# Two-layer hybrid encoder on one core: a new written-out order for the attention stage, with the first output tiles inside it

## What is computed

```python
xn = rms_norm(h, attn_norm_g[l])
q, k, v, u = jnp.split(xn @ w_in[l], splits, axis=-1)        # 512, 128, 128, 512 columns
q = apply_rope(rms_norm(q, q_norm_g[l]), cos, sin) * q_scale  # 8 heads of 64
k = apply_rope(rms_norm(k, k_norm_g[l]), cos, sin)            # 2 heads of 64
attn = sliding_sink_attention(q, k, v, sinks[l])              # chunks of 64, window 128, 16 global keys
pool = multiscale_pool(u, w_pool[l], pool_scale[l])           # 4 groups: trailing mean of 2/4/8/16 minus the token,
                                                              # then a 128x128 map for each group
h = h + jnp.concatenate([attn, pool], axis=-1) @ w_out[l]
xn = rms_norm(h, ffn_norm_g[l])                               # second sub-layer, not touched
h = h + (gelu(causal_dwconv(xn @ w_gate[l])) * (xn @ w_up[l])) @ w_down[l]
```

## Time and profile before

| | before |
|---|---|
| median of 3 runs | 1080.35 us (1080.12 to 1081.51) |
| the profiled execution's own time | 1079.61 us |
| its span | 1077.8 us |
| PE busy | 1044.7 us (97%) |
| PEld busy | 995.3 us (92%) |
| DVE busy | 683.9 us (63%) |
| ACT busy | 461.7 us (43%) |
| POOL busy | 106.5 us (10%) |
| mean granted TensorE clock | 0.988 of full speed |
| DMA | 94.94 MB, mean 88 GB/s |

### The profile page before, as it was taken

The page is one execution under the profiler, slowest core; times in us unless marked ns, Lnnn a source line. Parts: engine busy times, 40 slices in busy tenths (PEclk is TensorE's granted clock), DMA queues, the critical chain, the costliest instruction groups (busy, mean ns, idle before and its releaser), DMA issues.

```text
span 1077.8 us, 18641 instructions
## 1 busy us (share of the span) xinstructions
PE 1044.7 (97%) x7880; PEld 995.3 (92%) x7880; DVE 683.9 (63%) x1008; ACT 461.7 (43%) x698; POOL 106.5 (10%) x108
## 2 busy tenths in 40 slices
PE   7998899999999999999999988999999999999998
PEld 7887799999999999999999878999989999899987
DVE  6667645658946689455546576546698466984452
ACT  6775445334323343233338655354343333433322
POOL 1262000010000100000002610001000000000000
PEclk9989999999999999999999899999999999999999
DMA  7211222332232322322231112332313323133312
GB/s 231 80 49 40 79 79 79 92 105 79 79 118 80 118 79 79 118 79 88 89 99 40 50 40 79 100 97 78 114 44 118 118 84 112 41 123 113 98 59 78
DMA packets 94106, 94.94 MB, mean 88 GB/s; under 512 B 3424, under 2 KB 92856, under 8 KB 94024
## 3 DMA queue, kind: packets, MB, share of 16 engines
q1 hardware_dynamic: 93456, 93.58, 27.2%
q10 hardware_dynamic: 312, 0.18, 0.1%
q0 software_dynamic: 256, 0.01, 0.0%
HBM read 91.65 MB, written 2.10 MB: 87 GB/s over the span
## 4 chain that ended last, share of the span: by engine, by line
PE 78%; DVE 11%; ACT 8%; issue 3%; DMA 0%; POOL 0%; DVEq 0%; SPq 0%; ACTq 0%; POOLq 0%
PE slot L577 63%; PE slot L865 11%; ACT probs L1213 3%; PE slot L625 1%; ACT rot_s L1135 1%; DVE w_lo L430 1%; ACT w_hi L419 1%; DVE nmax L1550 1%; PE slot L925 1%; DVE h L1757 1%; DVE ms_work L1495 1%; DVE probs L1569 1%; DVE v_T L1470 1%; DVE mix_lo L1585 1%; DVE m_op_lo L1721 0%
## 5 line engine op out<-in xcount | busy, mean ns | idle before, releaser
L577 PE MATMUL slot<-x_hi,w_hi 128*128 128x264 f32 (+2 forms) x1520 | 355.9, 301 | 4.2 <-DVE u_sb L1532 2.9
L577 PE MATMUL slot<-x_lo,w_hi 128*128 128x264 f32 (+2 forms) x1520 | 352.3, 298 | 0.0
L577 PE MATMUL slot<-x_hi,w_lo 128*128 128x264 f32 (+2 forms) x1520 | 351.9, 298 | 0.0
L577 PEld LDWEIGHTS slot<-x_hi,w_hi 128*128 128x128 f32 x1520 | 248.1, 190 | 16.7 <-DVE u_sb L1532 4.3
L577 PEld LDWEIGHTS slot<-x_lo,w_hi 128*128 128x128 f32 x1520 | 246.7, 190 | 7.3
L577 PEld LDWEIGHTS slot<-x_hi,w_lo 128*128 128x128 f32 x1520 | 246.4, 190 | 7.5
L430 DVE TENSOR_TENSOR w_lo<-raw,w_hi 128x2048 fp32r<-128x2048 f32 (+1 forms) x70 | 157.2, 2246 | 90.0 <-ACT w_hi L419 90.0
L419 ACT ACTIVATE w_hi<-raw 128x2048 fp32r<-128x2048 f32 (+3 forms) x72 | 128.2, 1781 | 162.2 <-PE slot L577 113.3
L1029 POOL TENSOR_TENSOR work<-work 128x528 f32<-128x528 f32 (+1 forms) x32 | 41.9, 1309 | 712.3 <-DVE work L1681 350.6
L1283 ACT ACTIVATE work<-gate,par_all 128x528 f32<-128x528 f32 (+1 forms) x44 | 31.9, 731 | 135.1 <-DVE gate L1451 68.2
L865 PE MATMUL slot<-m_op_hi,w_hi 128*128 128x264 f32 (+1 forms) x256 | 73.8, 288 | 1.2 <-DVE h L1757 0.8
(11 more groups left out here) (195 smaller groups left out, 1627.8 us busy)
## 6 DMA issues: line engine op xcount, KB each, us to landing
raw<-in_w_gate SPq DMA_DIRECT2D x44, 512.0 KB, 4.7
raw<-in_w_up SPq DMA_DIRECT2D x44, 512.0 KB, 4.4
raw<-in_w_down SPq DMA_DIRECT2D x32, 512.0 KB, 4.2
raw<-in_w_in SPq DMA_DIRECT2D x19, 512.0 KB, 4.8
raw<-in_w_out SPq DMA_DIRECT2D x16, 512.0 KB, 4.0
raw<-in_w_down SPq DMA_DIRECT2D x16, 384.0 KB, 3.6
x_in<-in_x SPq DMA_DIRECT2D x4, 512.0 KB, 6.1
out<-y_out SPq DMA_DIRECT2D x4, 256.0 KB, 2.3
```

Of the source, the lines that this page charges most:

```text
L577: ins = nc.tensor.matmul(out_part, w[ws][:, r, cols], a[:, k, tokens], start=first and n == 0 and w is w_hi and a is a_hi, stop=end and w ...
```

## The change

The arithmetic is the same; the order in which PE, ACT and DVE do it is another, and it is written out call by call where loops and tables stood.

- **PE, ahead of attention.** Layer 1: rows 6 and 7 of k come with the first two rows of v between the products with the high and the low part of x. q1 moves to slot 0 and its first rows (three in layer 0, one in layer 1) go ahead of the transposes of v. u3's last rows mix with the first six rows of the side work.
- **PE, attention.** scores run one to three blocks ahead of the transposes; a transpose and the heads before it are no longer adjacent but have rows of side work between them; the side tiles and the pooling maps, now in halves (m3a to m0b), alternate between two spare areas, one in slot 2 and one in slot 3. The transposed meta columns move to a place in slot 3's first bank (`meta_T`), so probs_T(b) also waits for heads(b-2) to be read out.
- **PE, output.** Tiles out0 and out1 are cut into ten parts (`OUT_PARTS`), done among the last blocks; rows of heads 0 to 4 cover the first half of the tokens. Output unit 0 is split in two halves of rows on ACT and DVE.
- **ACT.** The order is by call: squares of q2, shift(3), squares of q3, split_hi of unit 4, q_rms(0), shift(4), q_rms(1), then the blocks. exps waits for the row maxima alone and does the sink's exponential last. Pooling maps are read out in halves.
- **DVE.** The order is by call; the one chain semaphore becomes two (`nm_steps`, `rden_steps`).

```diff
+FILL = [("u2a", KT), ("u2b", KT), ("u1a", KT), ("m3a", 1), ("m3b", 1), ("u1b", KT), ("u0a", KT), ("u0b", KT), ("m2a",
+        1), ("m2b", 1), ("m1a", 1), ("m1b", 1), ("m0a", 1), ("m0b", 1)]
+OUT_PARTS = [(0, (7, 6), (0, 1)), (0, (0, 1, 2, 3), (0,)), (1, (7, 6), (0, 1)), (1, (0, 1, 2, 3), (0,)), (0, (5,), (0, 1)),
+             (1, (5,), (0, 1)), (0, (4,), (0, 1)), (1, (4,), (0, 1)), (0, (0, 1, 2, 3), (1,)), (1, (0, 1, 2, 3), (1,))]
...
-        side = slot[3][:, 1, 0:HALF]
+        area = {4: slot[3][:, 1, 0:HALF], 5: slot[2][:, 1, 0:HALF]}
+        meta_T = slot[3][:, 0, 4 * CHUNK:4 * CHUNK + P]
...
                 if l > 0:
-                    project("k", U_KV, ready=lambda k: pe.wait_ge(xlo_ready, l * (2 * KT) + (k + 1)))
-                    project("v", U_KV)
+                    s = open_slot("k", l)
+                    pe.wait_ge(lo_split[U_KV % 2], slot_turn(l, U_KV) + 2)
+                    dense(s, U_KV % 2, 0, eight[0:6], x_hi, x_lo, last=False,
+                          ready=lambda k: pe.wait_ge(xlo_ready, l * (2 * KT) + (k + 1)))
+                    sv = open_slot("v", l)
+                    for part in (0, 1):
+                        if part == 1:
+                            dense(sv, U_KV % 2, P, eight[0:2], x_hi, x_lo, last=False)
+                        for k in (6, 7):
+                            pe.wait_ge((xhi_ready, xlo_ready)[part], l * (2 * KT) + (k + 1))
...
                 project("q0", U_Q)
+                s, ahead = open_slot("q1", l), 3 if l == 0 else 1
+                dense(s, U_Q % 2, P, eight[0:ahead], x_hi, x_lo, last=False)
                 s = open_slot("v_T", l)
...
                 column_mean("k_sq", l, block_mean, k_squares, headsq_ready, l * 5 + 1)
-                project("q1", U_Q)
+                dense(ps.slot("q1"), U_Q % 2, P, eight[ahead:], x_hi, x_lo, first=False).then_inc(filled[ps.slot("q1")], 1)
                 project("q2", U_Q + 1)
                 project("q3", U_Q + 1)
-                q_means(0)
-                project("u3", U_U23)
...
                     if b > 1:
                         pe.wait_ge(meta_out, l * (NB - 1) + (b - 1))
+                    if b > 1:
+                        pe.wait_ge(evac[ps.slot(f"heads{b - 2}")], ps.before(f"heads{b - 2}", l) + 1)
...
-                project_side(*side_rows(-1))
-                q_means(1)
-                for step in range(NB + 2):
-                    if step < NB:
-                        scores(step)
...
+                q_means(0)
+                u3_rows(0, 6)
+                fill(0, 2)
+                u3_rows(6, 7)
+                fill(2, 3)
+                u3_rows(7, 8)
+                fill(3, 6)
+                q_means(1)
+                scores(0)
+                fill(6, 8)
+                scores(1)
+                fill(8, 14)
+                scores(2)
+                fill(14, 16)
+                probs_T(0)
+                scores(3)
+                fill(16, 20)
+                probs_T(1)
+                fill(20, 25)
+                heads(0)
+                fill(25, 26)
+                scores(4)
...
+                fill(48, 51)
+                heads(4)
+                fill(51, 52)
+                probs_T(6)
+                fill(52, 53)
+                heads(5)
+                fill(53, 54)
+                fill_out(0)
+                probs_T(7)
+                fill(54, 55)
+                heads(6)
+                fill_out(1)
+                fill_out(2)
+                probs_T(8)
+                fill(55, 56)
+                heads(7)
+                fill_out(3)
+                fill_out(4)
+                heads(8)
+                fill_out(5)
+                fill_out(6)
+                fill_out(7)
+                fill_out(8)
+                fill_out(9)
...
-                    act.wait_ge(nm_ready, l * NB + b + 1)
+                    act.wait_ge(nm_steps, 3 * (l * NB + b) + 3)
...
-                shift(3)
-                split_hi(act, l, 4)
-                q_squares(2)
-                q_rms(0)
-                q_squares(3)
-                shift(4)
-                q_rms(1)
...
+                q_squares(2)
+                shift(3)
+                q_squares(3)
+                split_hi(act, l, U_U01)
+                q_rms(0)
+                shift(4)
+                q_rms(1)
+                exps(0)
+                exps(1)
...
+                split_lo(dve, l, U_U01)
+                scaled("u3", u_sb[:, 0, PAD:])
+                q_scales()
+                row_maxima(0)
+                u_half(0)
+                row_maxima(1)
+                divide(0)
```

More of the change, by code:

```diff
@@ new lines, in out_part @@
+                def out_part(t, rows, halves_of):
+                    unit, s = U_OUT, ps.slot(f"out{t}")
+                    for k in rows:
+                        if k >= 4:
+                            for half in range(2):
+                                name = half_name("m", k - 4, half)
+                                pe.wait_ge(evac[ps.slot(name)], ps.before(name, l) + 1)
+                        else:
+                            name = f"heads{4 if halves_of == (0,) else NB - 1}"
+                            pe.wait_ge(evac[ps.slot(name)], ps.before(name, l) + 1)
+                        for w, a in ((w_hi, mix_hi), (w_hi, mix_lo), (w_lo, mix_hi)):
+                            for half in halves_of:
+                                n, t0 = (TAIL_HALF, TAIL0) if l + 1 == DEPTH else (HALF, 0)
+                                ins = nc.tensor.matmul(slot[s][:, half, 0:n], w[unit % 2][:, k, t * P:(t + 1) * P],
+                                                       a[:, k, t0 + half * n:t0 + (half + 1) * n],
+                                                       start=k == 7 and w is w_hi and a is mix_hi,
+                                                       stop=k == 3 and w is w_lo, skip_group_check=True)
+                    return ins
@@ L1617, in _ @@
-                pool_map_lo(3)
+                split_lo(dve, l, U_U01)
[5 more added lines that the diff above has]
+                divide(0)
+                pooled_tile(0)
+                row_maxima(2)
+                divide(1)
+                split_lo(dve, l, U_POOL)
+                row_maxima(3)
+                u_half(1)
+                pooled_lo(0)
+                u_half(2)
@@ new lines, in _ @@
+                meta_probs_out(1)
+                pool_map_lo(0, 0)
+                heads_lo(0)
+                divide(2)
+                row_maxima(4)
+                pooled_tile(1)
+                meta_probs_out(2)
+                divide(3)
+                pool_map_lo(0, 1)
+                heads_lo(1)
+                row_maxima(5)
+                pooled_lo(1)
+                meta_probs_out(3)
+                u_half(3)
+                divide(4)
+                heads_lo(2)
+                row_maxima(6)
@@ new lines, in _ @@
+                meta_probs_out(4)
+                pooled_tile(2)
+                divide(5)
+                u_half(4)
+                heads_lo(3)
+                row_maxima(7)
+                pooled_lo(2)
+                meta_probs_out(5)
+                divide(6)
+                u_half(5)
+                pool_map_lo(1, 0)
+                heads_lo(4)
+                row_maxima(8)
+                meta_probs_out(6)
+                pool_map_lo(1, 1)
+                out_split_lo(4, 8, (outhi_split, l + 1), outlo_split)
@@ new lines, in _ @@
+                pooled_tile(3)
+                heads_lo(5)
+                divide(7)
+                pooled_lo(3)
+                pool_map_lo(2, 0)
+                meta_probs_out(7)
+                out_split_lo(0, 4, (hi_split[U_OUT % 2], slot_turn(l, U_OUT) + 1), lo_split[U_OUT % 2])
+                pool_map_lo(2, 1)
+                heads_lo(6)
+                divide(8)
+                meta_probs_out(8)
+                heads_lo(7)
+                pool_map_lo(3, 0)
+                pool_map_lo(3, 1)
```

350 lines of the change are left out of this document (185 added, 165 removed).

## The result

| | before | after |
|---|---|---|
| median of 4 runs each, side by side | 1080.78 us (1080.12 to 1081.51) | 1060.51 us (1058.99 to 1063.16) |
| the profiled execution, its span | 1079.61, 1077.8 us | 1060.28, 1057.7 us |
| mean granted TensorE clock | 0.988 | 0.995 |
| PE, DVE, ACT busy | 1044.7, 683.9, 461.7 us | 1037.7, 686.5, 464.1 us |

The ratio after to before is 0.9817 [0.9805, 0.9829]: 20.3 us are gained where 10.8 were forecast, outside the range on the fast side.

What follows compares the result with a forecast made beforehand. PE was taken as the bound, losing time in attention to waits and slow clock. Content 55.4 + waits 1.9 + slow clock 3.0 = 60.3 us per layer; gains 5.7 and 5.2, together 10.8, gave 1069.5 us, range 1062.5 to 1076.5.

Steps and rivals of the forecast that it cites:

- The gate of layer 0: Start of scores(0), waiting for q3's rotation on POOL; claimed to move by -0.1 us and stand at 69.5 to 69.7.
- v_T's wait: Layer 0, 1.93 us before the transposes of v; covering it with q1 matmuls claimed worth nothing unless the relay shortens.
- the stage: Attention from the start of scores(0) to the start of out2; claimed 60.3 us in either layer, from 65.9 and 64.5.
- four short waits: PE's waits left in attention: heads(0) 0.35, probs_T(6) 0.6, heads(5) 0.4, probs_T(7) 0.5; claimed 1.9 us together.
- The wait at u3: PE at product u3, ahead of attention, claimed to wait about 1.3 us behind a sparse q_means(0).
- the low clock kept as a constant: Slow PE clock behind the wait of some 2 us at scores(0); claimed to stay at 3.0 us in each layer.
- my first rival: Low clock falls earlier, at u3: 1066.5 to 1067.7 us for one layer, 1063.5 to 1066 for both; chance 0.22.
- The forecast's own course: Low clock behind the wait at scores(0) in both layers, 3.0 us each, giving 1069.5 us; chance 0.45.
- PE's content: PE's own attention work at full clock: dense 29.9, scores 7.9, heads 9.5, transposes 6.3, returns 1.8; sum 55.4 us.
- the front of layer 1: Layer 1 ahead of scores(0): covering k's 0.9 us wait for x_lo claimed to bring scores(0) the full 0.9 earlier.
- The relay: ACT and POOL work leading to scores(0): POOL's L992 held as long, ending 0.4 later; between -0.45 and +0.4, taken -0.1.
- The slower rival: A wait of 1.6 to 1.9 us mid-attention halves PE's clock, two such stretches per layer: 1086 us; chance 0.07.

Runs made afterwards that it cites:

- the second profile: The changed kernel run once more, nothing altered, for its spread: 1061.90 us.
- the kernel with the front alone: The kernel before with only k with v in layer 1 and q1's first rows ahead of the transposes of v: 1077.78 us, ratio 0.998.
- the kernel with both halves and unit 4 late: The changed kernel with q_means(0) inside q3, q_means(1) behind u3's last rows, five side rows before scores(0), unit 4 split behind the k chain: 1065.14 us.

## Why the prediction failed, step by step

**Right.** The gate of layer 0 hardly moved (69.71, and 69.26 in the second profile; forecast 69.5 to 69.7), and covering v_T's wait was worth nothing by itself. The waits left in the stage were walked at 1.9 us, "four short waits"; they are 1.7 in layer 0, and heads(5) 0.24, probs_T(6) 0.62 and probs_T(7) 0.34 are the named places (heads(0) did not wait; one block's scores did, for ACT to have read the slot, 0.4, and one matmul waited 0.2 for mix_lo). The wait at u3, forecast 1.3, is 1.2. There is no low clock between 78 and 130 us and no wait for x_lo or u_sb, and the waits for mix_lo at the heads are gone.

**The step that failed most: the low clock kept as a constant.** I carried 3.0 us per layer from the earlier trace rows "after a gate wait of some 2 us". In the profiled execution of layer 0 it fell at u3 instead, in PE's slack, which was my first rival: 3.0 too much. In layer 1 it fell there too and again behind the gate, but for 3.4 us instead of some 7, and the stage is 1.0 us longer than that of layer 0: 1.0 instead of 3.0. The runs show that this is not one outcome but several: the same program loses it behind the gate in one execution and at u3 in another. The forecast's own course does occur, and its size is nearer 2.5 than 3.0 (58.3 and 58.1 us of stage against 55.7); but even then the kernel takes 1063.57, not 1069.5. So the rival alone doesn't mend the forecast.

**The second: PE's content was too large.** Take the waits and the low clock out of the stages, and 55.7 - 1.7 = 54.0 and 56.6 - 1.8 - 1.0 = 53.8 us are left, where I had 55.4. Two terms are over-sized by the rows. Transposes I took at 0.70 and a way back of 0.11; from 94.98 to the dense matmul at 95.44 and its 0.1 of way back is 0.56. Two scores next to each other take 1.18 (92.61 to 93.79), where I had 2 x 0.89. Nine groups of transposes make 1.3 to 2.2, the one pair of scores 0.6. I had read the cost of the transposes from rows where the next piece was another small one, and then added the way back on top. The heads came out as carried (1.13 from 96.25 to the dense matmul at 97.38, for 1.12). Together the two terms are 1.9 to 2.8 us too large where 1.4 to 1.6 are missing, so something else was carried too small by 0.3 to 1.4; what it is isn't settled.

**The third: the front of layer 1** gave 1.9 us instead of 1.0. The k/v rows are 1.5 of it, where I had 0.9, the wait as it shows (54.63 against 53.15 with and without them, and 55.06 against 53.57 in the kernel before). The other 0.4, where I had 0.1, is what the change has there beyond the kernel with the front alone (53.57 against 53.15): the new order on ACT and DVE, and PE's u3 mixed with side rows.

In numbers, forecast less measured: layer 0 stage 60.3 - 55.7 = 4.6 (clock 3.0, content 1.4, waits 0.2), layer 1 stage 60.3 - 56.6 = 3.7 (clock 2.0, content 1.6, waits 0.1), front 0.9. The clock is 5.0 of it and content 3.0. Together these are 9.2 of the 9.3 us by which the span came out shorter than forecast. (The forecast's own 5.7 and 5.2 add to 10.9, where I wrote 10.8.)

**The relay.** I had POOL's product held as long as before, ending 0.4 later, and the gate moved by -0.1. It wasn't held at all: POOL started 0.46 us ahead of DVE's split. Nor did the long product set the gate before. POOL was done with it at 67.32 and then waited for ACT's shift(4):

```profile
68.04 0.32 POOL L996 TENSOR_TENSOR q_rot<-rot_c,rot_s 128x64 f32<-128x64 f32 x1 [0.72 <-ACT rot_s L1135]
```

So there were 0.7 us to spare, and the upper bound of +0.4 had no ground. ACT's shift(4) sets the gate in both kernels, at 65.22 for 65.30 in layer 0. The Trainium skill (GPSIMD Engine Reference, Specifications) speaks of contention with VectorE; the rows here say that it depends on which of the two starts first, and that the loser pays.

**The slower rival** had 0.07. Its mechanism is real: with the output parts last a wait of 2.2 us had 10 us at 0.50 behind it, in both layers. It starts from a wait that the walk did not have, and the walk was good to 0.2 us.

## What to carry to other kernels

A slow stretch is not a constant of a place: ask where narrow matmuls stand next to a wait, count each as a place where the clock may fall even if the wait is short, and price it by the slack behind it. Here 3.4 us at half clock cost nothing ahead of a gate that another engine sets, as long as PE waited there anyway, and 1.0 us behind it; 6.8 us cost 2.5 behind it. If PE must lose its clock, let it be ahead of the gate: moving the narrow matmuls away from the gate and filling its wait with dense rows was worth 2.2 us here, and opening the gate earlier was worth nothing. Read the price of a small piece from its start to the next dense matmul, the way back included, and only once.

## What the hardware showed that I had not expected

- The same program takes one of several courses. In layer 0 of its two profiles the low clock stands at u3 in one (0.78 from 60 to 65 us, 1.00 behind the gate) and behind the gate in the other (1.00 and 0.50), after nearly the same waits (1.19 and 1.16 us at u3). Where the narrow matmuls were moved from u3 the spread of four runs fell from 4 to 0.9 us. The Trainium skill (TensorE: Matmul & The Clock Gate, Part 1) calls the ramp at a kernel's start run-variable; the rows here show the like in the middle of a kernel.
- At u3, with the narrow matmuls right ahead of it and a wait of 1.1 to 1.2 us, the clock fell at 13 of 16 places (two layers in each of eight profiles); with the narrow matmuls elsewhere and the same wait it fell at none of eight.
- At the gate, with the narrow matmuls right ahead of it, the clock fell at 22 of 24 places, the kernel before among them: at all 15 with a wait of 0.8 us or more, and at seven of the nine with a wait of 0.5 us or none. With five dense rows between them and scores(0) it fell at none of eight, with waits of 0.4 us or none. So the wait of over 1 us that the expectations ask for isn't needed at the gate, and at equally short waits the place of the narrow matmuls makes the difference. The edit at the gate moves side rows as well as the narrow matmuls; moving those rows alone was not tried.
- DVE and POOL hold each other for whole instructions, where DVE reads two tiles in SBUF, be they ever so small: a product on DVE of 4 elements a partition took 1.05 us, where its like took 0.16 to 0.40, beside a POOL addition of 1.07 us in the kernel with both halves and unit 4 late.

```profile
69.75 1.07 POOL L1099 TENSOR_TENSOR run_a<-run_b 128x528 f32<-128x528 f32 x1
...
69.79 1.05 DVE L1675 TENSOR_TENSOR nmax<-nmax,q_scale 128x4 f32<-128x4 f32 x1
```
